# A hybrid conv / attention / MoE step on one core: a third buffer of gated rows, two stores held behind the first token gather, four more filler products, and gathers moved behind additions

## The reference

```python
x  = x + gate1 * (mixed @ w_o)
h2 = rms_norm(x, norm2_g) * (1 + scale2) + shift2
x  = x + gate2 * hier_moe(h2, ...)          # outputs y_prompt (128 rows), y_sample (512 rows)
# hier_moe: y = sum over the token's two experts e of  w_e * (silu(t @ w1[e]) * (t @ w3[e])) @ w2[e]
```

## Time and profile before

| | |
|---|---|
| median of 3 runs | 1187.36 us (1185.61 to 1188.19) |
| the profiled execution's own time | 1191.8 us |
| its span, first to last instruction | 1189.9 us |
| PE busy | 1141.5 us (96%) |
| VectorE, ScalarE, GpSimd busy | 573.0, 229.2, 398.3 us |
| mean granted TensorE clock | 0.988 |
| data moved by DMA | 200.88 MB, 185.20 MB of it on SyncE's queue (q1) |

### The profile page before, as it was taken

One profiled execution on the slowest core, in us unless ns is written; L12 is line 12 of the kernel. 1 busy time (PEld: TensorE's weight loads), 2 busy tenths in 40 slices (PEclk: granted clock), 3 DMA queues, 4 the chain that ended last, 5 costly groups with the idle time before them and its releaser, 6 DMA issues.

```text
span 1189.9 us, 15117 instructions
## 1 busy us (share of the span) xinstructions
PE 1141.5 (96%) x5942; PEld 720.0 (61%) x5943; DVE 573.0 (48%) x1133; ACT 229.2 (19%) x492; POOL 398.3 (33%) x346
## 2 busy tenths in 40 slices
PE   3999999999999999999999999999979999999995
PEld 1666777777777777777777777755534333333342
DVE  3564477455796794485445446536673121111121
ACT  4222356122571002001100010011120111111010
POOL 1475500469004454345444444000001132223242
PEclk9999999999999999999999999999989999999998
DMA  9955120022200222222222216441179999999962
GB/s 352 340 201 192 42 80 1 18 71 80 80 1 1 72 71 72 71 71 71 71 71 71 71 71 230 177 159 65 60 306 423 402 406 410 407 406 413 394 219 32
DMA packets 54039, 200.88 MB, mean 169 GB/s; under 512 B 5648, under 2 KB 6224, under 8 KB 47824
## 3 DMA queue, kind: packets, MB, share of 16 engines
q1 hardware_dynamic: 47056, 185.20, 40.4%
q0 software_dynamic: 6304, 13.13, 4.4%
q10 hardware_dynamic: 608, 1.58, 0.3%
HBM read 189.36 MB, written 18.91 MB: 175 GB/s over the span
## 4 chain that ended last, share of the span: by engine, by line
PE 81%; DMA 13%; DVE 2%; issue 1%; SPq 1%; ACT 1%; POOLq 0%; POOL 0%; ACTq 0%; DVEq 0%
PE psum L2425 30%; PE psum L2208 12%; PE psum L2512 5%; PE psum L2444 4%; DMA y_prompt<-arena,slot_rows_ctx 4%; PE psum L2329 4%; PE psum L2185 4%; PE psum L2389 3%; PE psum L2630 2%; DMA y_sample<-arena,slot_rows 2%; PE psum L2628 2%; DMA y_prompt<-arena,slot_rows_b_ctx 2%; PE psum L2661 2%; DMA y_prompt<-arena,slot_rows_q_ctx 2%; PE psum L2133 1%
## 5 line engine op out<-in xcount | busy, mean ns | idle before, releaser
L2425 PE MATMUL psum<-arena,weight_ring 128*128 128x320 f32 x864 | 238.7, 432 | 0.0
L806 POOL TENSOR_TENSOR weight_ring<-weight_ring 128x512 f32<-128x512 f32 x80 | 105.6, 1320 | 299.2 <-DMA weight_ring<-in_w_in 128.7
L2425 PEld LDWEIGHTS psum<-arena,weight_ring 128*128 128x128 f32 x864 | 163.1, 190 | 65.6
L2425 PE MATMUL psum<-x,weight_ring 128*128 128x320 f32 x480 | 133.1, 432 | 0.0
L2425 PEld LDWEIGHTS psum<-x,weight_ring 128*128 128x128 f32 x480 | 90.7, 190 | 37.0
L807 POOL TENSOR_TENSOR weight_ring<-weight_ring 128x512 f32<-128x512 f32 x80 | 110.3, 1379 | 0.0
L2208 PE MATMUL psum<-weight_ring,x 128*128 128x256 f32 x384 | 88.0, 380 | 0.0
L2208 PEld LDWEIGHTS psum<-weight_ring,x 128*128 128x128 f32 x384 | 71.7, 190 | 11.3 <-issue 1.9
L1625 DVE TENSOR_TENSOR arena<-psum,arena 128x320 f32<-128x320 f32 x96 | 45.8, 488 | 57.9 <-PE psum L2425 57.2
L2512 PE MATMUL psum<-weight_ring,arena 128*128 128x512 f32 x160 | 72.0, 597 | 0.5 <-DVE arena L1691 0.5
L2055 DVE SCALAR_TENSOR_TENSOR arena<-arena,ropeC 128x1024 f32<-128x1024 f32 x12 | 15.4, 1284 | 115.0 <-DMA y_prompt<-arena,slot_rows_b_ctx 78.3
(11 more groups left out here) (401 smaller groups left out, 1764.4 us busy)
## 6 DMA issues: line engine op xcount, KB each, us to landing
arena<-in_w SPq DMA_DIRECT2D x22, 2048.0 KB, 21.2
weight_ring<-in_w SPq DMA_DIRECT2D x21, 2048.0 KB, 19.4
weight_ring<-in_w_in SPq DMA_DIRECT2D x15, 2048.0 KB, 8.5
arena<-in_w_ada SPq DMA_DIRECT2D x6, 2048.0 KB, 12.5
x<-in_w SPq DMA_DIRECT2D x5, 2048.0 KB, 22.7
x<-in_x_sample SPq DMA_DIRECT2D x2, 2048.0 KB, 12.2
arena<-in_w_ada SPq DMA_DIRECT2D x4, 1024.0 KB, 14.4
weight_ring<-in_w_ada SPq DMA_DIRECT2D x4, 1024.0 KB, 14.7
```

The lines of the kernel that those rows point to most:

```text
L806: nc.gpsimd.tensor_tensor(out[:, 0:2], a_[:, 0:2], b_[:, 0:2], op)
L2425: last = mm(out, w[:, k, :], src[:, k, :], start=(k == 0), stop=(k == 3))
```

## The change

Four things are changed.

1. A third buffer of gated rows, in the place of the context tile of `x`. `slot_gates(n)` waits for the additions of result `n-3` instead of `n-2`; for result 2, the first in the new buffer, it waits until the store to `y_prompt` that reads this place has landed.
2. ScalarE issues its two stores (last `h2` tile, `y_prompt`) only when gather 0 has landed.
3. Gather `n+5` is written behind the additions of result `n` instead of ahead of them.
4. Fillers: 7 instead of 5 ahead of gather 0's transposes, and one each ahead of and behind gather 1's transposes. The wait for the bank that the new fillers write (`emptied(rank)`) moves ahead of them.

```diff
-        gated = [at(Z + 9216, 1024), at(9216, 1024)]
+        gated = [at(Z + 9216, 1024), at(9216, 1024), x_sb[:, 4 * D:5 * D]]
...
             for t in range(COUPLES - 1):
+                add_main(t)
                 gather_next(XG + 2 + out_main(t))
-                add_main(t)
                 if t % 2:
+                    add_half(t // 2)
                     gather_next(XG + 2 + out_half(t // 2))
-                    add_half(t // 2)
...
             act.wait_ge(s_h2, NT)
+            act.wait_ge(s_xg[0], 16)
             act.dma_start(h2_dram[P * CTX:P * NT, :], h2[:, CTX, :]).then_inc(s_last_h2out, 16)
             act.dma_start(io["y_prompt"], x_sb[:, D * CTX:D * NT]).then_inc(s_last_outx, 16)
...
             def slot_gates(n, tile):
-                if n >= 2:
-                    added = 16 * sum(adds_before[m] for m in range(n - 1))
+                if n == 2:
+                    dve.wait_ge(s_last_outx, 16)
+                if n >= len(gated):
+                    added = 16 * sum(adds_before[m] for m in range(n - len(gated) + 1))
                     dve.wait_ge(s_put_lat, added)
                     dve.wait_ge(s_put_ctx, added)
...
-            keep_busy(5, 1)
+            keep_busy(7, 1)
             emptied(pe, INDEX[("route", NT - 1)])
...
+            emptied(pe, INDEX[("rank", NT - 1)])
+            keep_busy(1, 4)
             next_tokens(1)
-            emptied(pe, INDEX[("rank", NT - 1)])
+            keep_busy(1, 4)
             half_gate_up(0)
```

More of the change, by code:

```diff
@@ L926, in add_rows @@
                     pool.wait_ge(s_put_lat, 16 * added[0])
-                nc.gpsimd.indirect_dma_start(io["y_sample"], bass.IndirectOffsetOnAxis(ap=lat, axis=0), gated[n % 2][lo:hi, :], None,
+                nc.gpsimd.indirect_dma_start(io["y_sample"], bass.IndirectOffsetOnAxis(ap=lat, axis=0), gated[n % len(gated)][lo:hi, :], None,
                                              bounds_check=N_LAT - 1, oob_is_err=False, compute_op=add).then_inc(s_put_lat, 16)
@@ L930, in add_rows @@
                     pool.wait_ge(s_put_ctx, 16 * added[0])
-                nc.gpsimd.indirect_dma_start(io["y_prompt"], bass.IndirectOffsetOnAxis(ap=ctx_, axis=0), gated[n % 2][lo:hi, :], None,
+                nc.gpsimd.indirect_dma_start(io["y_prompt"], bass.IndirectOffsetOnAxis(ap=ctx_, axis=0), gated[n % len(gated)][lo:hi, :], None,
                                              bounds_check=N_CTX - 1, oob_is_err=False, compute_op=add).then_inc(s_put_ctx, 16)
@@ L2050, in slot_gates @@
             def slot_gates(n, tile):
-                if n >= 2:
-                    added = 16 * sum(adds_before[m] for m in range(n - 1))
+                if n == 2:
+                    dve.wait_ge(s_last_outx, 16)
+                if n >= len(gated):
+                    added = 16 * sum(adds_before[m] for m in range(n - len(gated) + 1))
                     dve.wait_ge(s_put_lat, added)
                     dve.wait_ge(s_put_ctx, added)
-                V.scalar_tensor_tensor(out=gated[n % 2], in0=gate2[:, 1, :], scalar=is_ctx[:, tile:tile + 1], in1=gate2[:, 0, :],
+                V.scalar_tensor_tensor(out=gated[n % len(gated)], in0=gate2[:, 1, :], scalar=is_ctx[:, tile:tile + 1], in1=gate2[:, 0, :],
                                        op0=mult, op1=add).then_inc(s_gate, 1)
@@ L2061, in rows_made @@
                     dve.wait_ge(s_d, 2 * n + half + 1)
-                    part = gated[n % 2][:, 512 * half:512 * (half + 1)]
+                    part = gated[n % len(gated)][:, 512 * half:512 * (half + 1)]
                     V.tensor_tensor(part, psum[:, 3072 + 512 * half:3584 + 512 * half], part, mult).then_inc(s_prod, 1)
```

## The result

The changed kernel takes 1190.63 us (median of 17 runs), the kernel before 1186.78 in the same job. The ratio is 1.0036, with a 95% interval of 1.0027 to 1.0044: slower by 3.2 to 5.2 us. One of the changed kernel's 17 runs took 1728.72 us at a granted clock of 0.655 and is not in the ratio; nothing on record shows why. I had forecast 1186.3, with 1181.5 to 1190.6 as the range.

A forecast was written before the change was run, and what follows sets the result against it. PE and DMA engines are both full in the mixture of experts, so gains come only where PE stands or runs slowly. Early part and late gathers put PE at +2.6, third buffer -3.7: -1.1, 1186.3 us, range 1181.5 to 1190.6.

The forecast's parts named there:

- All the signs that I named: Transposes at about 881.4, no half clock around 885 and 914, no VectorE wait near 1097, waits for gathers 7 and 10.
- The third buffer ... -3.7 at 1101: At about 1099 us PE's 2.1 us wait for VectorE goes, and the slow clock behind it gives 1.6 back.
- PE is at -4.1: Behind gather 1 PE is 4.1 us earlier, by held stores and fillers; bounds -1.3 and -5.1.
- That costs 1.0: PE is at -2.9: Held stores delay couple 0's second up matrix to 896.1, PE comes at 895.1; its lead shrinks from 3.9 us.
- I take c = 1.7: Chain of additions gains 1.7 us because gather 5 no longer lies in GpSimd's DMA queue ahead of the first additions.
- My bounds were 0 and 5.5: Limits of the chain's gain from gather 5: nothing, or the 5.5 us one gather holds the queue.
- The late gathers: PE stands 2.7 us for gather 7 and 1.6 for gather 10, with clock losses of 1.6 and 0.8.
- The half price for the clock behind the second stand: Behind the 1.6 us stand for gather 10, only half of 1.6, 0.8 us, is charged for slow clock.
- gather 5's place is worth 5.5: Rival: gathers hardly late since gather 5's queue place gives its full 5.5 us; end -4.1, 1183.3 us; chance 0.21.
- The held h2 store: Rival: the held store of the last `h2` tile makes gather 1 late; +3.2, 1190.6 us; chance 0.15.
- the last rival: Holding the stores does nothing: gather 0 lands at 883.24 as now; +1.7, 1189.1 us; chance 0.12.
- the gathers are not late at all: Rival: gathers land within about 5 us of issue, before PE wants tiles 7 and 10; -7.8, 1179.6 us; chance 0.05.

The follow-up runs named there:

- experiment 2: Kernel before with the gathers behind the additions and nothing else: 1192.52 us, 1.0050 to the kernel before.
- experiment 3: Kernel before with the third buffer and nothing else: 1186.03 us, 0.9987 to the kernel before.
- experiment 5: Kernel before, unchanged, profiled a second time: start 45.72 us, middle 252.78 us.
- experiment 13: Kernel before, unchanged, profiled a third time: start 45.53 us, middle 253.97 us.
- experiment 14: Kernel before, unchanged, profiled a fourth time: start 45.62 us, middle 253.05 us.
- experiment 1: Changed kernel with the gathers ahead of the additions again, other three edits kept: 1184.39 us, 0.9981 to the kernel before.
- experiment 10: Changed kernel with gathers ahead and neither store held, third buffer and all fillers kept: 1184.13 us, 0.9985 to the kernel before.
- experiment 7: Changed kernel with gathers ahead and the y_prompt store only behind the first silu: 1183.42 us, 0.9982 to the kernel before.
- experiment 12: Changed kernel, gathers ahead, y_prompt store behind first silu, half fillers ahead of first table and last rank: 1183.20 us, 0.9966 to the kernel before.
- experiment 8: Changed kernel with three fillers ahead of tile 7's transposes and two ahead of tile 10's: 1192.74 us, 1.0050 to the kernel before.
- experiment 11: Changed kernel, gathers ahead, h2 store issued at once, y_prompt store behind first silu: 1184.40 us, 0.9985 to the kernel before.

## Why the prediction was wrong

The mechanism of the loss was in the forecast: GpSimd issues in order, gathers behind additions come late, gather 7 and then gather 10. All the signs that I named for it came: tile 0's transposes at 881.89, no half clock around 885 and 914, no wait for VectorE, stands for gathers 7 and 10. They show the path and not its price. The steps that failed are sizes of the sum: against the loss I set two gains that were too large, the third buffer and the start, and the loss itself was a little too small.

Piece by piece, the second profile of the changed kernel set against the mean of the second to fourth of before gives: ahead of the last rank -1.29 (the change does not touch it, and these starts lie anywhere from 872.8 to 875.2 in all profiles), start -1.56, middle +6.86, tail -0.12, together +3.9; the times say +3.2 to +5.2. Without the piece that the change does not touch it is +5.2, and the misses below add up to it: -1.1 + 2.9 (third buffer) + 2.5 (start) + 1.0 (late gathers) = 5.3. The two first profiles, both without a fall at 873, give another split: +0.08, -0.73, +4.51, -0.42, together +3.4. There the buffer's 3.7 were real, and the miss lies in the start (-0.73 for -4.1) and the late gathers.

*"The third buffer ... -3.7 at 1101".* The wait is gone, as said. But 2.1 us with a fall of the clock behind it was one execution's; in three others it was 0.2, 1.4 and 0.5 without a fall, and the buffer wins 0.8. By the usual profiles this is the largest miss, 2.9. I noted that the execution was 4.4 above the median and took those 4.4 off the sum as if they lay nowhere. They lay in the two places that I read the gains from.

*"PE is at -4.1" behind gather 1.* For like cases the start is 1.6 shorter (44.06 against 45.62). In the execution that I read, the clock had not fallen at 873, and PE stood 3.93 us ahead of gather 0. With the code unchanged up to there, it fell between 871.2 and 873.9 in 10 of the 15 profiles that have this code. Then the fillers run at half clock and cover most of the gather's wait anyway, in before too: 1.5 to 2.4 us are left of 3.9 (experiments 2, 3, 5, 13, 14). The Trainium skill ("TensorE: Matmul & The Clock Gate", What's actually happening) says that the window in which TensorE's activity is watched runs on freely and does not begin anew when a kernel starts; that the clock falls here in one execution of the same code and not in the next (10 of 15) fits that, and no run here shows the cause.

*"That costs 1.0: PE is at -2.9"*, the second up matrix. Its size as a stand was right: it landed at 896.65 (I had said 896.1), and PE stood 1.35. I gave it no clock, though I charged clock behind the gathers; the up product of couple 0 took 10.07 us, where the profile of experiment 1 has 7.09. So in that execution the held stores gave back at 896 what they had won at 882, which is why the start is 47 with them and without them (experiment 10), and 42.5 to 42.9 where the matrix is in time (7 and 12).

*"I take c = 1.7"*, the chain's gain from gather 5 leaving its place. From the first addition to gather 8 it took 68.3 us. To gather 7 behind the additions, in GpSimd's rows of the changed kernel's first and second profile:

```profile
950.28 1.50 POOL L927 DMA_INDIRECT y_sample<-arena,slot_rows  x1 [20.03 <-DVE arena L2066]
...
1017.78 1.04 POOL L894 DMA_INDIRECT arena<-h_scratch,slot_rows  x1 [0.30 <-issue]
```

```profile
946.21 1.50 POOL L927 DMA_INDIRECT y_sample<-arena,slot_rows  x1 [20.58 <-DVE arena L2066]
...
1017.79 1.82 POOL L894 DMA_INDIRECT arena<-h_scratch,slot_rows  x1 [0.31 <-issue]
```

That is 67.5 and 71.6: c is 0.8 and -3.3, and in experiments 2 and 8 the chain took 67.6 and 71.0. My bounds were 0 and 5.5; below nothing I did not look. But -3.3 is not gather 5's doing: with the gathers ahead too, the stretch from the first addition to gather 8 took 68.3 to 69.8 us in eight profiles and 71.4 to 71.5 in three (experiments 10 to 12). Chains of two speeds come with either order, and beside the quick ones c is about 1.2, beside the slow ones nothing. Why some are slower stays open.

*The late gathers.* I charged 2.7 + 1.6 + 1.6 + 0.8 = 6.7; measured are 8.3 and 7.7 (260.77 and 260.13 less 252.47). The latencies were right: gathers 7 and 10 took 14.1 and 14.7 us from issue to landing (13.4 and 13.8 forecast). The half price for the clock behind the second stand was wrong; it fell behind 1.95 us as behind 3.03.

*The rivals.* That gather 5's place is worth 5.5 falls with c. The held h2 store did not hold gather 1: it landed 8.9 us after its issue, where more than 13.7 would have been needed. Holding the stores did bring gather 0 forward (7.1 to 7.8 us against 9.3 to 10.0 from issue to landing), so the last rival's reason is wrong, though no gain shows in the times (experiment 10). That the gathers are not late at all falls by the latencies above. I had written that no gather shown lands in under 13.4 us; gather 1 of before took 11.0. By the Trainium skill's fit ("DMA: Bandwidth & Descriptors", Anatomy of one DMA, SWDGE path), an estimate of 3.2 us for 512 KB, they would have been in time; no gather here, not even gather 0 with the stores held, landed in under 7 us.

## What to carry to other kernels

Before a gain is read off one profile, see where that execution stands among the runs; if it is above the median, the excess lies at definite places, and a wait that may or may not drop the clock is the first suspect. Price every new stand with the slow stretch that may follow it. Work that is queued behind a chain of read-modify-write transfers takes on the chain's pace; moving two items of it to the front only passed the lateness on to others here.

## What the runs showed of the hardware

- The clock fell at 871 to 874 us in 10 of 15 executions with the same instructions up to there, and later, at 882 to 896, in all of the others but one. With the changed fillers the start took 43.93 to 44.06 us in five executions with the early fall, and 47.05 to 47.24 in three without it that lost the clock later; what decides between them no run shows.
- Between 895 and 1135 us the clock fell in, or up to 1.6 us behind, stands of PE of 1.35, 1.85, 1.95, 2.07, 2.13, 2.73, 3.03, 4.16 and 5.51 us, for 3.41 or 6.83 us. It did not behind stands of 0.8, 1.1 and 1.4. The stand of 1.16 us ahead of the first half tile was followed by a fall in two profiles of the code before (the first and the fourth) and not in four others, so a stand's length alone does not decide it.
- The two late gathers, or the one, cost 8.3 and 7.7 us in two profiles of the same kernel: stands of 3.03 and 1.95 us with two slow stretches of 3.41, or one stand of 5.51 us with one of 6.83.
- Gather 0 took 7.1 to 7.8 us with the stores held (eight profiles), 9.3 to 10.0 beside them (seven profiles); one 512 KB store beside it instead of two did not shorten it (9.8).
